# Removing the meeting point between head loop and GLU, and loading the S5 outputs behind the last S5 store

## What is computed

```
u = rmsnorm(h, norm_g[l])
proj = u @ w_in[l]
o_a = gated_deltanet(qkv_a, beta_raw, a_raw, ...)
p_a = (o_a * silu(z_a)) @ w_br_a[l]
# s5_layer, after the scan over time:
y = y.reshape(bsz, s, S5_WIDTH) + d * xf
y = gelu(y)
val, gate = split(y @ w_glu, 2, axis=-1)
o_b = val * sigmoid(gate)
p_b = (o_b * silu(z_b)) @ w_br_b[l]
merged = gates[:, :, 0] * p_a + gates[:, :, 1] * p_b + gates[:, :, 2] * p_c
h = h + merged @ w_out[l]
return rmsnorm(h, final_g)
```

## Time and profile before

| | |
|---|---|
| median of 3 runs | 2095.52 us (2095.28 to 2096.42) |
| the profiled execution: its own time | 2096.82 us |
| its span, first to last instruction | 2095.1 us |
| mean granted clock of PE | 0.998 |
| PE busy | 2064.7 us, 99% |
| DVE, ACT, POOL busy | 61%, 39%, 36% |
| DMA | 260.63 MB, mean 124 GB/s |

### The profile page before, as it was taken

One profiled execution on the slowest core, in us unless ns is written; L12 is line 12 of the kernel. 1 busy time (PEld: TensorE's weight loads), 2 busy tenths in 40 slices (PEclk: granted clock), 3 DMA queues, 4 the chain that ended last, 5 costly groups with the idle time before them and its releaser, 6 DMA issues.

```text
span 2095.1 us, 30759 instructions
## 1 busy us (share of the span) xinstructions
PE 2064.7 (99%) x12124; PEld 1689.8 (81%) x12124; DVE 1270.9 (61%) x1787; ACT 808.6 (39%) x1064; POOL 748.2 (36%) x555
## 2 busy tenths in 40 slices
PE   6999999999999999999999999999999999999998
PEld 6799888887787887878878788777778888888886
DVE  6554353439689596895968959676433335454333
ACT  5433232353444533445344453353242222232223
POOL 0000000038586585765858658577201000100000
PEclk9999999999999999999999999999999999999999
DMA  8244343453343433434334343343356555553334
GB/s 258 61 127 134 102 134 91 114 135 91 104 115 96 119 99 104 114 96 118 99 104 114 96 119 98 104 118 103 104 170 206 173 183 151 181 150 110 112 124 148
DMA packets 382913, 260.63 MB, mean 124 GB/s; under 512 B 23769, under 2 KB 351810, under 8 KB 382146
## 3 DMA queue, kind: packets, MB, share of 16 engines
q1 hardware_dynamic: 364146, 203.16, 35.6%
q0 software_dynamic: 11408, 43.00, 6.0%
q10 hardware_dynamic: 7232, 12.72, 1.6%
HBM read 223.17 MB, written 27.28 MB: 120 GB/s over the span
## 4 chain that ended last, share of the span: by engine, by line
PE 90%; DVE 4%; ACT 2%; DMA 2%; issue 1%; POOLq 0%; ACTq 0%; DVEq 0%
PE bank L460 28%; PE bank L462 27%; PE bank L461 27%; DVE wl L454 1%; PE bank L1102 1%; DVE lb L2057 1%; PE bank L995 1%; PE bank L983 1%; DMA yst<-s_out 1%; ACT wh L446 0%; PE bank L1050 0%; PE bank L1064 0%; PE bank L1039 0%; DVE tl L2123 0%; DMA raw<-in_w_kv_mem_dram 0%
## 5 line engine op out<-in xcount | busy, mean ns | idle before, releaser
L460 PE MATMUL bank<-uh,wh 128*128 128x512 f32 x2048 | 823.2, 402 | 4.0 <-DVE wl L454 3.7
L462 PE MATMUL bank<-uh,wl 128*128 128x512 f32 x2048 | 799.3, 390 | 0.0
L461 PE MATMUL bank<-ul,wh 128*128 128x512 f32 x2048 | 799.1, 390 | 0.0
L454 DVE TENSOR_TENSOR wl<-raw,wh 128x1024 fp32r<-128x1024 f32 x352 | 467.7, 1331 | 476.6 <-ACT wh L446 475.3
L446 ACT ACTIVATE wh<-raw 128x1024 fp32r<-128x1024 f32 x352 | 369.9, 1058 | 554.3 <-DMA raw<-in_w_in_dram 184.9
L460 PEld LDWEIGHTS bank<-uh,wh 128*128 128x128 f32 x2048 | 384.7, 188 | 92.2 <-issue 11.3
L462 PEld LDWEIGHTS bank<-uh,wl 128*128 128x128 f32 x2048 | 384.5, 188 | 83.3
L461 PEld LDWEIGHTS bank<-ul,wh 128*128 128x128 f32 x2048 | 385.2, 188 | 72.2
L626 POOL DMA_DIRECT2D gated_c<-ox x8 | 4.3, 543 | 372.5 <-DVE ox L1820 371.8
L667 POOL TENSOR_TENSOR hr<-tcos,gr 128x512 f32<-128x512 f32 x32 | 51.7, 1615 | 199.4 <-DVE gi L2154 199.2
L1454 ACT ACTIVATE gk<-bank 128x512 f32<-128x512 f32 x48 | 28.7, 598 | 189.6 <-PE bank L462 189.5
(11 more groups left out here) (360 smaller groups left out, 2835.9 us busy)
## 6 DMA issues: line engine op xcount, KB each, us to landing
raw<-in_w_in_dram SPq DMA_DIRECT2D x224, 512.0 KB, 3.8
raw<-in_w_kv_mem_dram SPq DMA_DIRECT2D x32, 512.0 KB, 3.9
raw<-in_w_out_dram SPq DMA_DIRECT2D x32, 512.0 KB, 3.6
gates<-gk ACTq DMA_DIRECT2D x48, 256.0 KB, 4.3
gates<-gates POOLq DMA_DIRECT2D x24, 512.0 KB, 4.6
raw<-in_s_w_glu_dram SPq DMA_DIRECT2D x16, 512.0 KB, 4.0
raw<-in_w_br_c_dram SPq DMA_DIRECT2D x16, 512.0 KB, 4.0
raw<-in_w_br_a_dram SPq DMA_DIRECT2D x16, 512.0 KB, 3.9
```

Source lines behind the costliest of these rows:

```text
L454: dve.tensor_tensor(k.wl[slot][:, c], k.raw[slot][:, c], k.wh[slot][:, c].bitcast(F32), ALU.subtract).then_inc(k.w_lo, 1)
L460: pe.matmul(o, ah, bh, start=start, stop=False)
L461: pe.matmul(o, ah, bl, start=False, stop=False)
L462: return pe.matmul(o, al, bh, start=False, stop=stop)
```

## The change

- `end_phase` and the semaphore `phase_end` go. PE loses its drain behind G11 and its wait before the GLU; ACT, DVE and POOL lose drain and wait.
- POOL gets `load_s5`: in the last `mixer`, directly behind the last `store_s5` and ahead of `store_head`, it waits until all eight S5 stores have landed and starts the 2 MB load of `yst`. It no longer waits for `y_st` behind the loop; its waits for the stores of z_b and of the gated heads stay ahead of the first load of `zv`.
- `onesr` moves to the front of its area, so `yst` no longer lies over it. Tiles behind the new place, up to the old one, move by 512 bytes.
- ACT waits for `og` (the last head's gating, on DVE) ahead of the Gelu.

```
+            k.onesr = sb(area, "onesr", [P], F32R)
             k.qraw = sb(area, "qraw", [S + 3])
...
-            k.onesr = sb(area, "onesr", [P], F32R)
...
-def end_phase(k, e, n):
-
-    e.drain().then_inc(k.phase_end, 1)
-    e.wait_ge(k.phase_end, 4 * n)
...
+        def load_s5():
+            pool.wait_ge(k.y_st, 16 * HEADS)
+            pool.dma_start(k.yst[:, :, :], k.y_d.rearrange("(t p) s -> p t s", p=P)).then_inc(k.y_in, 16)
+
...
         if l: store_s5()
+        if not j: load_s5()
...
     pool.wait_ge(k.zb_st, 16 * HEADS)
-    pool.wait_ge(k.y_st, 16 * HEADS)
     pool.wait_ge(k.g_st, 16 * HEADS)
-    end_phase(k, pool, 1)
-
-
-    pool.dma_start(k.yst[:, :, :], k.y_d.rearrange("(t p) s -> p t s", p=P)).then_inc(k.y_in, 16)
...
     mixer((HEADS + 1, 0), None, (HEADS, -1), 2)
-    pe.drain().then_inc(k.phase_end, 1)
     for b in range(4):
         big((HEADS + 1, 0), 2 + b, *range(8))
-    pe.wait_ge(k.phase_end, 4)
...
     mixer((HEADS + 1, 0), None, (HEADS, -1), gate=PER, blocks=2)
-    end_phase(k, act, 1)
...
     split_hi(k, act, B_GT + 14, halves=[0])
+    act.wait_ge(k.og, 2 * HEADS)
     act.wait_ge(k.y_in, 16)
...
     mixer((HEADS + 1, 0), None, (HEADS, -1), 2, False)
-    end_phase(k, dve, 1)
```

More of the change, by code:

```diff
@@ L291, in build @@
             sems("sp_waits", "pe_waits", "pool_waits", "w_hi", "w_lo")
-        k.w_used, k.phase_end = \
-            sems("w_used", "phase_end")
+        k.w_used, = \
+            sems("w_used")
         k.w_in_half = sems("w_in0", "w_in1", "w_in2", "w_in3")
```

## The result

| | before | with the change |
|---|---|---|
| median of 16 runs | 2095.49 us (2094.74 to 2096.42) | 2099.87 us (2099.04 to 2101.23) |
| the profiled execution, its span | 2096.82, 2095.1 us | 2099.56, 2097.9 us |
| PE busy | 2064.7 us | 2066.2 us |

The ratio is 1.0021, 95% interval 1.0015 to 1.0028: the change makes the kernel 4.4 us slower, where +0.6 us was forecast. The time lies inside the range of 2093.0 to 2100.3, 0.9 us above the forecast's own band (2094.1 to 2099, chance 0.67), and just beyond the 4.2 us that were set as the limit of "same"; an end beyond it on the slow side had a chance of 0.06. The interval, 3.1 to 5.9 us, leaves open on which side of 4.2 us the change lies.

A forecast was written before the change was run, and what follows sets the result against it. PE, busy 99% of the span, was taken as the bound, so only its waits count: 2.3 us gained at the seam, 2.9 lost at the output norm, +0.6 on the median, 2096.1 us; range 2093.0 to 2100.3.

The forecast's parts named there:

- landing minus 1510.2: Output norm: PE stalls by the landing time of G12's second weight half minus 1510.2 us, nothing if it lands earlier.
- rival B: Output norm: G12's weights wait for the whole yst load, 11.9 us; stall 7.0 us, time 2100.3; chance 0.05.
- Landing: 1513.0, stall 2.8 us: G12's second weight half: 2.62 MB at 325 GB/s from 1504.5, plus 0.4 us, giving a 2.8 us stall at the norm.
- the earlier case: Weight load issued at 1529.02 beside yst before the change: 11.9 us, landing 0.9 us after full traffic ended.
- 2.9: Output norm: PE's predicted loss in us, a 2.8 us stall plus 0.1 for slower first starts.
- All three late starts: PE's delays at G12, G13 and G14's second half: 0.49, 0.27 and 1.55 us, all forecast to go, 2.3 us.
- rival C: G14's second half: something other than yst keeps ACT busy, 1.55 us stay lost; time 2097.6, chance 0.05.
- so I add the difference to the median: Final sum: seam waits taken as independent of the profiled run's 1.3 us excess, so +0.6 us on 2095.52 gives 2096.1.
- The drain's 0.49: PE's drain between G11 and G12 at the meeting point: 0.49 us lost, forecast to go.
- G13's 0.27 us: PE's late start of G13, whose split on ACT the meeting held: 0.27 us lost, forecast to go.
- Rival A: Output norm: transfers barely hinder each other, weights land by 1511; stall 0 to 0.8 us, time 2093.2 to 2094.1; chance 0.20.
- Rival D: Moved tiles or later traffic that no longer meets: a gain beyond PE's starts, time under 2091.3; chance 0.02.

The follow-up runs named there:

- The first two runs: Changed kernel with the yst load moved behind the store of zk, 2094.24 us; changed kernel with sqh ahead of G12's second split on ACT, 2093.98 us.
- the load behind the store of zk: Changed kernel with the 2 MB load of yst issued behind the store of zk instead of the last S5 store: 2094.24 us, ratio 0.9994.
- half-early kernel: Changed kernel with the yst load in two, 1 MB behind the last S5 store, the rest behind the store of zk: 2093.67 us, ratio 0.9993.
- the kernel with the swap: Kernel loading half of yst early, with DVE writing sql before key scales and differences in the last two mixer calls: 2094.90 us, ratio 0.9998.

## Why the prediction was right or wrong

**Right: the place and the chain.** The load of yst collides with the second half of G12's weights, and ACT's strict order carries that to sqh, sql and the output norm. The first two runs show it from both ends: without the collision the stall goes, and with the collision but another order on ACT it goes as well. The rule "landing minus 1510.2" came out to 0.1 us: the landing of 1513.65, put 0.64 us later for the shift between the profiles, gives 4.1 us, and 4.05 was measured. So the forecast of a stall at this place is no luck; that the time fell inside the range owes something to its width, as its upper end came from rival B.

**Mis-sized: the landing.** The step "Landing: 1513.0, stall 2.8 us" should have said 1514.3, in the time of the profile before, and 4.1 us. I took two transfers, 2.62 MB, and left out the store of G10's gates, 256 KB, which is issued at 1507.81 and took 5.7 us. An estimate with it: 2.88 MB at 325 GB/s end at 1513.4, and with the 0.9 us of lag that the earlier case had, instead of the 0.4 that I took, the landing is 1514.3. This fits, but it was worked out afterwards and no run took the store away. Other splits of the 1.3 us fit as well: the traffic ran at 303 GB/s from 1503 to 1513, and the next half of weights was issued at 1511.02, while this one was still on its way. The load of yst began well before the weights and still held them for 5 us.

**Missing: the clock.** The steps priced a stall at its length plus 0.1 us. One of 4 us also cost 1.6 us of half clock, with or without the early load; one of 1.6 us did not. The Trainium skill, "TensorE: Matmul & The Clock Gate", section "HAM oscillation — how this bites in real kernels", says that waits for transfers can send the engine back to its slow clock, so that the next matmuls start cold. The trace agrees: 0.50 of the granted clock from 1517 to 1520 us, though here it fell only 0.6 us after PE had resumed. The prediction looked for what PE waits for and not for what a wait does to the matmuls behind it. 4.16 + 1.6 stands where 2.9 stood.

**Right in the profile, perhaps too large in time: the gain.** All three late starts went, 2.3 us in the profile, and rival C was wrong: the Gelus started as soon as ACT got to them. By medians, the kernels without any stall at the norm or the seam gain only 1.2 to 1.5 us, but with intervals of 2 us on either side, so 2.3 isn't excluded. The step in doubt is "so I add the difference to the median": the terms came from a profiled execution that was 1.3 us above the median, and I took that excess for something outside the seam. With a gain of 1.4 instead of 2.3 and a loss of 5.8 the sum is +4.4, as measured; but the 1.4 is taken from the runs, so this is a fit and no test. With 2.3 the sum is +3.5, which lies inside the interval too.

**Wrong: two terms as a sum.** The drain's 0.49 and G13's 0.27 us are not independent. Since the change removes both, it did no harm to this sum; in a kernel that removes the drain alone the term was worth nothing that the medians show, and 0.3 us in the profile.

**The rivals.** Rival B gave nearly the measured time, 2100.3, but by another way: a landing at 1517 and a stall of 7 us. The landing was three us earlier, and the clock made up most of the rest, so that it nearly met the time is luck. Rival A was wrong for 2 MB; what it describes, weights that land in time, came with 1 MB. Rival D, a gain beyond what PE's starts show, found nothing for it in any run.

## What to carry to other kernels

When a transfer is moved to a quiet moment, don't ask whether the moment is quiet but which transfer starts within its duration, and then follow that one's consumer in its engine's order: the price is paid by the first instruction behind it that someone else is waiting for, here a 0.6 us copy that wanted none of the late data. Put such an instruction ahead of the wait, or split the load so that its first part is through in time. Price a stall of several us on the matrix engine with the slow matmuls behind it, and don't add up two waits in a row on one engine before asking whether the second grows when the first goes.

## What was not expected of the hardware

- After some 4 us without work at the output norm (4.05, 4.05, 4.06 and 4.21 us late in four profiles) PE's granted clock fell to 0.50, and matmuls started 0.43 instead of 0.23 us apart. In three of the profiles this lasted for about eight matmuls, in the fourth for 14, so the same stall costs 1.6 to 3 us on top. In two of them the clock fell before PE resumed, in the other two 0.6 and 1.3 us after it had. After 1.56 us at the same place it did not fall; after 2.85 us at another place, in the kernel with the swap, it did.
- A load of 512 KB took 3.6 to 4.9 us in these traces where no load of yst was in flight, 9.0 when it was issued 3.2 us behind one of 2 MB, and 4.4 when it was issued about as far behind one of 1 MB. With more transfers in flight, 3.3 us behind the 2 MB were 12.2 us (the load behind the store of zk), and 3.3 us behind the second 1 MB of the half-early kernel 6.2. So the distance behind the big load and its size don't set the delay by themselves.
